# Residual stream, norms and three projections with tokens on partitions, in a one-core encoder layer

## The reference, cut to what matters

```python
def layer_step(x, ...):
    hn = rms_norm(x, g_pre_mix)
    z, xbc, dt_raw, q, k, v = jnp.split(hn @ w_in, IN_SPLITS, axis=-1)
    ...                                   # conv, chunked scan, rotary, differential attention
    mix = jnp.concatenate([y_ssd, y_att], axis=-1) @ w_out
    h = x + rms_norm(mix, g_post_mix)
    qx = (rms_norm(h, g_pre_x) @ wq_x).reshape(bsz, l, MEM_HEADS, MEM_HEAD_DIM)
    ...                                   # cross-attention into 256 memory tokens, gives ox
    h = h + rms_norm(ox @ wo_x, g_post_x)
    hn = rms_norm(h, g_pre_ffn)
    f = (jax.nn.silu(hn @ w_gate) * (hn @ w_up)) @ w_down
    return h + rms_norm(f, g_post_ffn), ...
```

## Time and profile before

| | us |
|---|---|
| three runs | 2273.3, 2280.39, 2289.25 |
| median | 2280.39 |
| span of the profiled execution, first to last instruction | 2271.3 |
| the profiled execution's own time | not given apart; the lowest run is 2.0 above the span, the median 9.1 |
| TensorE busy | 2025.8 (89%) |
| VectorE, GpSimd, ScalarE busy | 958.1, 611.1, 517.5 |
| mean granted TensorE clock, as a share of 2.4 GHz | 0.938 |

### The profile page before, as it was taken

The page is one execution under the profiler, slowest core; times in us unless marked ns, Lnnn a source line. Parts: engine busy times, 40 slices in busy tenths (PEclk is TensorE's granted clock), DMA queues, the critical chain, the costliest instruction groups (busy, mean ns, idle before and its releaser), DMA issues.

```text
span 2271.3 us, 29479 instructions
## 1 busy us (share of the span) xinstructions
PE 2025.8 (89%) x12075; PEld 1916.1 (84%) x12075; DVE 958.1 (42%) x1622; ACT 517.5 (23%) x1073; POOL 611.1 (27%) x292
## 2 busy tenths in 40 slices
PE   5998999877688789799998977999999999999996
PEld 3998899866577679689888967999999999999994
DVE  5253304686676542740434374223313322331336
ACT  3300012265466532321323232100000000000002
POOL 3245535231000013312002331414332331433230
PEclk8999999997678989899998998999999999999998
DMA  4222322111400421001440121101111110111122
GB/s 152 85 91 96 107 89 86 33 62 38 144 1 1 153 103 38 29 24 66 160 149 20 38 93 39 54 29 56 37 37 38 38 56 20 56 38 34 42 102 83
DMA packets 61881, 148.52 MB, mean 65 GB/s; under 512 B 3904, under 2 KB 32960, under 8 KB 60224
## 3 DMA queue, kind: packets, MB, share of 16 engines
q1 hardware_dynamic: 33936, 103.53, 13.3%
q10 hardware_dynamic: 27824, 43.24, 5.6%
HBM read 123.31 MB, written 23.44 MB: 65 GB/s over the span
## 4 chain that ended last, share of the span: by engine, by line
PE 65%; issue 12%; DVE 12%; ACT 5%; POOL 3%; DMA 3%; SPq 0%; POOLq 0%; ACTq 0%; DVEq 0%
PE bank L213 19%; PE bank L216 18%; PE bank L217 18%; DMA w_raw<-in_wall 2%; POOL w_hi L445 2%; PE bank L875 1%; DVE at_sm L1606 1%; POOL w_lo L447 1%; PE bank L886 1%; DVE NLf L256 1%; PE bank L845 1%; PE bank L247 1%; DVE hid_l L1839 1%; DMA V<-out_v 1%; DVE E L1540 1%
## 5 line engine op out<-in xcount | busy, mean ns | idle before, releaser
L445 POOL TENSOR_TENSOR w_hi<-w_raw,one 128x1024 fp32r<-128x1024 f32 x130 | 253.6, 1951 | 1485.5 <-PE bank L213 1345.4
L216 PE MATMUL bank<-NL,w_hi 128*128 128x384 f32 x1824 | 618.3, 339 | 0.0
L213 PE MATMUL bank<-NH,w_hi 128*128 128x384 f32 x1632 | 556.3, 341 | 34.1 <-DVE hr L1837 14.4
L217 PE MATMUL bank<-NH,w_lo 128*128 128x384 f32 x1632 | 552.9, 339 | 0.0
L216 PEld LDWEIGHTS bank<-NL,w_hi 128*128 128x128 f32 x1824 | 346.7, 190 | 1.2
L213 PEld LDWEIGHTS bank<-NH,w_hi 128*128 128x128 f32 x1632 | 309.9, 190 | 37.0 <-DVE hr L1837 15.0
L447 POOL TENSOR_TENSOR w_lo<-w_raw,w_hi 128x1024 fp32r<-128x1024 f32 x130 | 330.4, 2542 | 10.2
L217 PEld LDWEIGHTS bank<-NH,w_lo 128*128 128x128 f32 x1632 | 309.5, 190 | 0.0
L1837 DVE TENSOR_TENSOR hr<-sg,bank 128x384 f32<-128x384 f32 x66 | 36.6, 555 | 431.8 <-PE bank L217 431.8
L213 PE MATMUL bank<-hid_h,w_hi 128*128 128x384 f32 x528 | 179.2, 339 | 16.2 <-DVE ACC L1848 14.6
L213 PE MATMUL bank<-w_hi,NH 128*128 128x256 f32 x576 | 165.5, 287 | 31.1 <-issue 14.6
(11 more groups left out here) (303 smaller groups left out, 2974.2 us busy)
## 6 DMA issues: line engine op xcount, KB each, us to landing
w_raw<-in_wall SPq DMA_DIRECT2D x130, 512.0 KB, 3.3
H<-in_xT SPq DMA_DIRECT2D x6, 1536.0 KB, 11.5
cK<-in_cmk SPq DMA_DIRECT2D x8, 1024.0 KB, 6.9
cV<-in_cmv SPq DMA_DIRECT2D x8, 1024.0 KB, 4.8
scratch_h<-H ACTq DMA_DIRECT2D x3, 1536.0 KB, 6.2
Hback<-scratch_h ACTq DMA_DIRECT2D x3, 1536.0 KB, 10.6
out_y<-Hback ACTq DMA_DIRECT2D x3, 1536.0 KB, 6.0
Kb<-in_kc SPq DMA_DIRECT2D x6, 512.0 KB, 9.4
```

The costliest lines, as they stand in the source:

```text
L213: m = mm(out, ah, bh, start=(i == 0), stop=False)
L216: mm(out, ah, bl, start=False, stop=False)
L217: m = mm(out, al, bh, start=False, stop=(i == n - 1))
L445: pool.tensor_tensor(whi[s][:], raw[s % 2][:], bc(one[:, 0:1], [P, WI]), ALU.mult).then_inc(w_hi, 1)
```

## The change

The residual stream, all norms, and the outputs of `w_out`, `wo_x` and `w_down` now lie with tokens on partitions: `[128, 9, 1024]`, nine tiles of 128 tokens. A sum over a token's features is then a sum along the free axis: ScalarE's square pass also accumulates it into one column of `stat`, and root and reciprocal work on 128x1. Gains become rows, loaded with a copy for every partition (`gB0`, `gB1`, 512 KB each). Because the following projection wants features on partitions, TensorE turns each normed tile with eight 128x128 transposes into banks 6 and 7, from which ScalarE makes the high and VectorE the low part. The squares-times-ones matmuls go.

`w_out` and `wo_x` become 36 units (`join_unit`: four column groups of 256 by nine tiles) of 24 matmuls of 128x256. A `down` group becomes 18 units of 6 matmuls of 128x512. Cross-attention writes its output as high and low parts at once (`OH`, `OL`). `H` is stored to `scratch_h` in the first join and loaded back whole as `H2` after cross-attention. The first projection's kinds go v, q, k, z. The end works tile by tile: ScalarE statistics, VectorE scale, GpSimd's addition of the residual, SyncE's store.

```diff
+        def pre_stat(act, z, src, junk, done):
+            alink(act, act_f(junk, src, ACT.Square, accum_out=col(S_N, z)))
+            act_f(col(S_N, z), col(S_N, z), ACT.Sqrt, bias=eps6[:, :], scale=1.0 / D).then_inc(done, 1)
+        def pre_scale(dve, z, src, out, gain):
+            dve.wait_ge(p_std, z + 1)
+            dlink(dve, nc.vector.reciprocal(col(S_N, z), col(S_N, z)))
+            STT(out=out, in0=src, scalar=col(S_N, z), in1=gain, op0=ALU.mult, op1=ALU.mult).then_inc(p_xn, 1)
+        def pre_trans(pe, z, src):
+            pe.wait_ge(p_xn, z + 1)
+            for j in range(2):
+                if z:
+                    pe.wait_ge(p_lo, 2 * z - 1 + j)
+                for i in range(4):
+                    m = nc.tensor.transpose(B[6 + j][:, tok(i)], src[:, tok(4 * j + i)], ident)
+                m.then_inc(p_tr, 1)
+        def join_unit(pe, item, base, n, ah, al):
+            jj, t = divmod(n, NT)
+            s = 2 * (jj % 2)
+            if t == 0:
+                pe.wait_ge(w_ready, item + 2 * jj + 2)
+            if n >= 4:
+                pe.wait_ge(j_ev, base + n - 3)
+            three(B[n % 4][:, 0:WC], ...)
...
+        def join_dve(dve, pair, mix, res, hi, lo, z0):
+            for n in range(27):
+                join_gain(dve, 36 * pair, n, mix)
+            for t in range(NT):
+                join_gain(dve, 36 * pair, 27 + t, mix)
+                join_sum(dve, pair, t)
+                if t >= 1:
+                    pre_scale(dve, z0 + t - 1, res[:, t - 1, :], mix[:, t - 1, :], g("gB1")[:])
+                join_add(dve, pair, t, mix, res)
+                if t >= 2:
+                    pre_lo(dve, z0 + t - 2, hi[:, :, tok(t - 2)], lo[:, :, tok(t - 2)])
+            pre_scale(dve, z0 + NT - 1, res[:, NT - 1, :], mix[:, NT - 1, :], g("gB1")[:])
+            for t in (NT - 2, NT - 1):
+                pre_lo(dve, z0 + t, hi[:, :, tok(t)], lo[:, :, tok(t)])
...
@@ sync
-            sp.dma_start(g("H")[:, :, cs(0)], xT[:, :, cs(0)]).then_inc(ld["x0"], 16)
+            sp.dma_start(ident, consts[:, C_ID:C_ID + P]).then_inc(ld["id"], 16)
+            for t in range(3):
+                sp.dma_start(g("H")[:, t, :], x_in[tok(t), :]).then_inc(ld_x[t], 16)
+                if t < 2:
+                    sp.dma_start(raw[t][:], wall[t]).then_inc(w_raw[t], 16)
...
@@ tensor
+                    if kind + jj == 0 and t + 2 < NT:
+                        pre_trans(pe, Z_X + t + 2, g("H")[:, t + 2, :])
...
+            for n in range(4 * NT):
+                if n < NT:
+                    pe.wait_ge(yl_s, n // 3 + 1)
+                join_unit(pe, I_WO, 0, n, YH, NL)
+                if n >= 27 + 2:
+                    pre_trans(pe, Z_J1 + n - 29, g("MIX")[:, n - 29, :])
+            for q in range(24):
+                ...
+                lin_unit(pe, I_WQ, 0, q, YH, NL)
+                if q < 2:
+                    pre_trans(pe, Z_J1 + 7 + q, g("MIX")[:, 7 + q, :])
...
@@ scalar
+            act.wait_ge(ld["res"], 32)
+            for n in range(4 * NT):
+                join_act(act, 1, n, g("MIX2"), g("H2"), OH, Z_J2)
...
@@ vector
+            dve.wait_ge(ld["gB0"], 64)
+            for t in range(NT):
+                for q in (2 * t, 2 * t + 1):
+                    add_down(NG - 1, q, B[q % 6])
+                if t:
+                    last_scale(t - 1)
```

More of the change, by code:

```diff
@@ L51, with build @@
 C_END = 1098
[L53 to L58, removed]
+G_MEM, G_PREMIX, G_POSTMIX, G_PREX, G_POSTX, G_PREF, G_POSTF = range(7)
+V_CW = 0
+V_CB = 32
+V_SSM = 40
+V_SUB = 44
+V_END = 45
+S_N, S_Q, S_V, S_END = 0, 40, 76, 96
 R_DTB, R_ALOG, R_DSK, R_LAM = 0, 8, 16, 24
 R_END = 280
-def build(nc, xT, memT, wall, wdt, consts, vecs, rows, kc, vc, h0, sconv, cmk, cmv,
+def build(nc, x_in, mem_in, wall, wdt, consts, vecs, gains, rows, kc, vc, h0, sconv, cmk, cmv,
           y_o, k_o, v_o, ssm_o, conv_o, mk_o, mv_o, zs_d, q_d, h_d):
@@ L173, in build @@
         ident = cst[:, C_ID:C_ID + P]
-        ld = {n: sem("ld_" + n) for n in ("cst", "vec", "row", "mem", "x0", "x1", "x2", "wdt", "scv", "h0", "Hb0", "xr")}
+        ld = {n: sem("ld_" + n) for n in ("par", "one", "res", "gB0", "gB1", "id")}
+        ld_x = [sem(f"ld_x{i}") for i in range(5)]
         w_raw = [sem(f"w_raw_in{i}") for i in range(2)]
@@ L240, in pre_pe @@
[L240 to L260, removed]
@@ new lines, in join_sum, with join_std, join_add @@
+        def join_sum(dve, pair, t):
+            q = S_Q + 4 * t
+            nc.vector.tensor_reduce(col(S_V, NT * pair + t), stat[:, q:q + 4], AX, ALU.add).then_inc(j_var, 1)
+        def join_std(act, pair, t):
+            n = NT * pair + t
+            act.wait_ge(j_var, n + 1)
+            act_f(col(S_V, n), col(S_V, n), ACT.Sqrt, bias=eps6[:, :], scale=1.0 / D).then_inc(j_std, 1)
+        def join_add(dve, pair, t, mix, res):
+            n = NT * pair + t
+            dve.wait_ge(j_std, n + 1)
+            dlink(dve, nc.vector.reciprocal(col(S_V, n), col(S_V, n)))
+            dve.wait_ge(j_ev, 36 * pair + 27 + t + 1)
+            STT(out=res[:, t, :], in0=mix[:, t, :], scalar=col(S_V, n), in1=res[:, t, :], op0=ALU.mult,
+                op1=ALU.add).then_inc(j_res, 1)
@@ L479, in _ @@
                 split(n, n % 4, False)
+            pool.wait_ge(ld["res"], 48)
+            for t in range(NT - 1):
+                pool.wait_ge(e_t, t + 1)
+                hb = g("Hback")[:, t, :]
+                pool.tensor_tensor(hb, hb, g("ACC")[:, t, :], ALU.add).then_inc(e_y, 1)
         @block.tensor
@@ L996, in tm_out @@
                     act.wait_ge(st_out[j % 4], 16)
-                for t in range(NT):
-                    n = tm_no(kind, jj, t)
-                    act.wait_ge(tm_mm, n + 1)
-                    act_f(g(f"stg{j % 4}")[:, t, :], B[(9 * jj + t) % 6][:, 0:256], f).then_inc(tm_ev, 1)
+                for t in range(start, NT):
+                    tm_evac(kind, jj, t, f)
                 store(kind, jj)
```

589 lines of the change are left out of this document (273 added, 316 removed).

## The result

| | us |
|---|---|
| kernel before, median of 4 runs | 2279.88 (2273.3 to 2289.25) |
| changed kernel, median of 4 runs | 2182.45 (2176.71 to 2184.99) |
| ratio, 95% interval | 0.9566 (0.9539 to 0.9592) |
| span of the profiled execution, before and after | 2271.3 and 2183.2 |

The change saves 97 us by the medians, 88.1 by the two profiled executions: that of before was one of the quicker runs, that of after the slowest of its four (2184.99).

The account below looks back on a forecast made before the run. The prediction took TensorE, with 65% of the chain, as the bound, winnable where it waits: start, two joins, end. Terms −20 − 12 − 19 + 0 − 7 − 21 = −79 took 2280 to 2201 us; range 2170 to 2255.

Parts of the forecast that it names:

- cross-attention: Cross-attention, writing its output as high and low parts at once: predicted 0 us, range 0 to +3.
- Start (−20): Kernel start: first projection matmul at about 19 us, ninth unit's end at 57 instead of 77.4; −20 us (−24 to −8).
- First join (−12): First join: VectorE sets the pace at 5.5 us a tile; 232 us against 243.8, so −12 (−18 to 0).
- The round trip: Joins' last column group: handshakes between ScalarE, VectorE and TensorE might set the pace; 1.1 us a tile allowed on VectorE.
- Second join (−19): Second join: same sum as the first join plus a reload stall; 240 us against 258.8, so −19 (−26 to −5).
- I book 6 for the stall and its refill: Second join's beginning: TensorE does four units, then waits for the reloaded residual and gain rows; 6 us booked.
- FFN (−7): FFN loop: less wait for the bank at each `down` group, 5.7 us in ten groups, plus pitch; −7 (−11 to −2).
- End (−21): Kernel end: norm tile by tile at 3.85 us a tile, 43 to 44 us instead of 65.0; −21 (−27 to −10).
- A (clock): Rival, joins and start: stretches mixing transposes with matmuls run at 1.2 GHz; 2268 us, chance 0.08.
- B (reload): Rival, second join and end: the reload comes at 155 GB/s, not 376; 2228 us, chance 0.10.
- C (GpSimd): Rival, joins' last column groups: GpSimd splits weights all the time, slowing VectorE's 1024-wide passes to 2.8 us; 2253 us, chance 0.08.
- D (gain rows): Rival, start, second join and end: each 512 KB gain takes 47 us to land; 2359 us, slower, chance 0.07.

## Why the prediction was right, point by point

**Direction, and where the time comes from: right.** Five stages gain, all within 6 us of their terms, and cross-attention loses 3.1 (0 to +3).

**Start (−20): right in total.** First matmul at 20.5 for the predicted 19, the ninth copy at 53.7 for 57, since a set of transposes costs 0.80 and not 1.29. (The 1.29 was the length of the row at 572.86; the matmul behind it began 1.13 later.) That is −23.7 there and −29 at the xBC projection (313.8 for 342.9); 9 us less remains at the first join. From first matmul to first join the same code of the kernel before took 789.9 in its own profile and 799.6 in the one with the loop written out, the changed kernel 786.9 to 793.8 in its versions. So these 9 us are no larger than what that stretch varies by. With the gain rows loaded later the stretch is as long as without (789.5 and 789.4), so they are not the cause; what is, is not shown. No experiment undid the order by tiles at the start: there the rows alone speak for it.

**First join (−12): right, pace shown.** VectorE sets the pace: doubling one of its passes costs 24 us, doubling TensorE's transposes under half of that. The round trip, which the prediction named as the way to be wrong, adds some 0.3 a tile, the wait for ScalarE's root. With the norms behind the last column group the join is as long as before. The pace was put at 5.5 and measured 4.75, because the handshakes cost less than the 1.1 allowed: 8 x 0.75 = 6, of which the total shows 2. The slower pitch in `wq_x` (0.1767 for 0.1745, 576 times) takes 1.3 of the rest; the other 3 are about the 2.75 that the last set of transposes but one (938.41), inside `wq_x`, waits for VectorE's low part.

**Second join (−19): right, one term mis-sized.** The stall ("I book 6 for the stall and its refill") was 8.8 us, the faster tiles made up for it. The step behind it, that neither ScalarE nor VectorE starts before the reload, was true of the code and not needed: moving the wait makes the join 7.9 us shorter still, 6.5 by the medians.

**FFN (−7): the term that was mis-sized, −12.7.** It held the shorter wait for the bank, booked at 5.7. The step went from some 1.9 to 1.26, and less the pitch itself that is about 0.75 each, 7.5 in ten groups. It lacked two things of opposite sign. The back-edge gaps: three steps of 2.6 to 3.1, and a slower clock behind each (0.50 from 1733 to 1736; the groups behind them took 51.4 to 52.2 for 50), some 14 us in the profile, of which writing out the loop gave 10.7 by the medians. And the pitch: the gate and up matmuls of 128x384 have 0.1767 in the changed kernel and 0.1733 to 0.1747 in nearly all groups before, 288 of them in each of the nine groups of this stage give 5 to 9 us of loss; 128x512 has 0.2343 for the assumed 0.2317, 2 to 3 us more.

The Trainium skill, page "Runtime: NRT & Kernel Launch", section "Instruction fetch mechanics", gives TensorE's instruction memory as 2048 instructions, filled in blocks of 256, and says that a taken branch to a target outside the current window of two pages forces a fetch before execution goes on. The runs agree that a jump back can bring a fetch and a stall: bodies of 1807 and 1843 instructions are fetched again, 9 fetches in an iteration, at three of the four jumps of the one and at all four of the other. They do not agree with a window of two pages, 512 instructions by an estimate from the page's blocks: bodies of 1651 and 1747 are far longer and are not fetched again. Seven of the page's blocks, 1792 by an estimate from it, would lie between; why not eight, no run here shows.

**End (−21): right, −24.1.** A tile takes 3.63 for the predicted 3.85. With the additions first it is 23 us slower, about the whole gain; as in the join, what the cheaper arithmetic gives beside the order is not separated.

**The rivals.** A (clock): the granted clock is 0.97 in both joins. In the last column group, where transposes stand behind every unit, it is 1.00 in the second join (1281 to 1311) and 0.94 in the first (900 to 930), there 0.84 from 899 to 910, where TensorE had just waited 3.2 us for the first scale, and 1.00 from 910 to 931. So the rule that the prediction cites beside A doesn't describe transposes among matmuls; it was the kernel with the norms behind that fell to 0.60. B (reload): 4608 KB in 18.0 us, 262 GB/s, between the 376 that the forecast took and B's 155; with the gain rows ahead of it the forecast had 17.4. C (GpSimd): the scale in the joins has a median of 1.285 us and a longest of 3.07, and 4 of 18 are over 1.3, so few collide. C's price takes the booked 6 off once for two joins: off twice, it is 46 and 2247, and A's terms give 66, not 67. D (gain rows): landed after 9.9 us by the median, far from the 27 where it decides.

## What to carry to other kernels

Here a norm over a token's features gained from tokens on partitions because a tile of 128 tokens can be finished beside the matmuls of the next: undo that order and the join is as long as before. Its arithmetic counts where VectorE sets the pace: one more pass of 1.28 us a tile cost the two joins 22. So look for the engine whose rows leave no gap (here VectorE, but for a short wait every second tile), and put each wait where its data is first read, not at the head of the stage. In a long hardware loop count TensorE's instructions, weight loads included: 192 more in the body cost 17 to 19 us here, while the first 96 of them brought no gap.

## What the runs showed that was not expected

- The same matmul of 128x384 has a steady pitch of 0.1733, 0.1747 or 0.1767 us at a granted clock of 1.00. In the kernel before it is 0.1767 in the xBC projection and mostly 0.1733 or 0.1747 in the FFN, with the same operands; in the changed kernel and all ten of its variants the FFN has 0.1767 throughout, which neither version of the kernel before has. The cause stays open; it is worth up to 10 us.
- An operation of VectorE with one input in a bank isn't slowed by GpSimd (0.64 each at the end, beside an addition of 2.40), one with both inputs in SBUF is, up to 3.4 for 1.28.
